# Both layers' S5 discretisation in the first steps, and the second MLP half squared on ScalarE

## What is computed

```python
proj = jnp.einsum('btd,de->bte', x, w_in)
...
mixed = jnp.concatenate([o_hg, o_rt, y5], axis=-1).astype(x.dtype) @ w_out
x = _layer_norm(ALPHA * x + mixed, ln1_w, ln1_b)
ff = jnp.square(jax.nn.relu(x @ w_up)) @ w_down
x = _layer_norm(ALPHA * x + ff, ln2_w, ln2_b)
```

```python
dt = jnp.exp(log_dt.astype(f32))[:, None]
mag = jnp.exp(dt * a_re)
ab_re = mag * jnp.cos(dt * a_im)
ab_im = mag * jnp.sin(dt * a_im)
den = a_re * a_re + a_im * a_im
nr = ab_re - 1.0
g_re = (nr * a_re + ab_im * a_im) / den
g_im = (ab_im * a_re - nr * a_im) / den
```

## Time and profile before

| | before |
|---|---|
| runs | 800.65, 802.97, 808.24 us |
| profiled execution | 800.36 us |
| its span | 798.3 us |
| TensorE matmul busy | 749.8 us (94%) |
| VectorE busy | 545.5 us (68%) |
| ScalarE busy | 380.1 us (48%) |
| mean granted TensorE clock | 0.972 |

### The profile page before, as it was taken

The page is one execution under the profiler, slowest core; times in us unless marked ns, Lnnn a source line. Parts: engine busy times, 40 slices in busy tenths (PEclk is TensorE's granted clock), DMA queues, the critical chain, the costliest instruction groups (busy, mean ns, idle before and its releaser), DMA issues.

```text
span 798.3 us, 17719 instructions
## 1 busy us (share of the span) xinstructions
PE 749.8 (94%) x7318; PEld 692.2 (87%) x7318; DVE 545.5 (68%) x1041; ACT 380.1 (48%) x727; POOL 41.9 (5%) x54
## 2 busy tenths in 40 slices
PE   5999789999999999989969899999999999999994
PEld 4888668879999999989969797778799999999994
DVE  7975872257788898884665987423478886666574
ACT  3513123435578654446448413233357874555442
POOL 4000012100000000000030001010000000000001
PEclk9999889999999999999999999999899999999998
DMA  8532122517355455444533222323354556555541
GB/s 337 188 110 79 36 71 98 211 50 221 122 159 186 159 173 194 145 151 158 166 126 106 82 82 81 123 81 114 109 171 154 176 180 187 178 169 183 186 132 55
DMA packets 31008, 113.56 MB, mean 142 GB/s; under 512 B 3568, under 2 KB 3776, under 8 KB 30544
## 3 DMA queue, kind: packets, MB, share of 16 engines
q1 hardware_dynamic: 28368, 101.83, 39.9%
q0 software_dynamic: 1984, 9.52, 3.1%
q10 hardware_dynamic: 576, 1.08, 0.4%
HBM read 108.24 MB, written 4.18 MB: 141 GB/s over the span
## 4 chain that ended last, share of the span: by engine, by line
PE 54%; DVE 21%; ACT 7%; issue 5%; DMA 1%; ACTq 0%; DVEq 0%
PE stream L998 11%; PE stream L1023 10%; PE stream L1024 10%; PE stream L1025 10%; DVE w_low L1526 8%; ACT w_high L1076 4%; PE mix L928 2%; DVE h_full L2070 1%; PE mix L899 1%; DVE h_low L2074 1%; PE mix L749 1%; ACT h_high L1418 1%; DMA w_raw<-in_weights 1%; PE mix L890 1%; PE mix L672 1%
## 5 line engine op out<-in xcount | busy, mean ns | idle before, releaser
L1526 DVE TENSOR_TENSOR w_low<-w_raw,w_high 128x1024 fp32r<-128x1024 f32 x153 | 187.3, 1224 | 92.6 <-ACT w_high L1076 91.0
L1076 ACT ACTIVATE w_high<-w_raw 128x1024 fp32r<-128x1024 f32 x153 | 161.3, 1054 | 113.3 <-PE stream L1025 94.8
L1023 PE MATMUL stream<-h_high,w_high 128*128 128x264 f32 x512 | 147.0, 287 | 1.4 <-issue 0.6
L998 PE MATMUL stream<-X,w_raw 128*128 128x264 f32 x560 | 138.1, 404 | 9.2 <-DMA w_raw<-in_weights 8.6
L1023 PE MATMUL stream<-a_high,w_high 128*128 128x264 f32 x456 | 135.3, 297 | 11.0 <-DVE a_low L2103 6.3
L1024 PE MATMUL stream<-h_low,w_high 128*128 128x264 f32 x512 | 145.1, 283 | 0.0
L1025 PE MATMUL stream<-h_high,w_low 128*128 128x264 f32 x512 | 145.0, 283 | 0.0
L998 PEld LDWEIGHTS stream<-X,w_raw 128*128 128x128 f32 x560 | 108.4, 198 | 32.2 <-DMA w_raw<-in_weights 9.0
L1024 PE MATMUL stream<-a_low,w_high 128*128 128x264 f32 x456 | 131.4, 288 | 0.0
L1025 PE MATMUL stream<-a_high,w_low 128*128 128x264 f32 x456 | 131.1, 287 | 0.0
L1023 PEld LDWEIGHTS stream<-a_high,w_high 128*128 128x128 f32 x456 | 87.8, 193 | 15.3 <-issue 14.0
(11 more groups left out here) (383 smaller groups left out, 1040.7 us busy)
## 6 DMA issues: line engine op xcount, KB each, us to landing
w_raw<-in_weights SPq DMA_DIRECT2D x192, 512.0 KB, 3.5
mats<-in_matrices POOLq DMA_DIRECT2D x2, 1024.0 KB, 5.9
S_hg<-in_state_hg POOLq DMA_DIRECT2D x2, 768.0 KB, 8.2
out_hg_s<-S_hg POOLq DMA_DIRECT2D x2, 768.0 KB, 3.7
consts<-in_constants POOLq DMA_DIRECT2D x1, 1484.5 KB, 9.4
X<-in_xT ACTq DMA_DIRECT2D x4, 264.0 KB, 5.3
out_y<-X SPq DMA_DIRECT2D x4, 264.0 KB, 2.1
S_rt<-in_state_rt POOLq DMA_DIRECT2D x2, 512.0 KB, 9.7
```

The costliest lines, as they stand in the source:

```text
L998: mm = pe.matmul(bnk[:, 0:T], w_raw[:, n % RAW_SLOTS, 128 * k:128 * k + 128], x[:, k, :], start=(kk == 0), stop=(kk == 7))
L1023: pe.matmul(bnk[:, 0:width], wh, xh, start=(first and kk == 0), stop=False)
L1076: act.activation(w_high[:, n % SPLIT_SLOTS, :], w_raw[:, n % RAW_SLOTS, :], ACT.Copy).then_inc(high_ready, 1)
L1526: put(tt(w_low[:, n % SPLIT_SLOTS, :], w_raw[:, n % RAW_SLOTS, :], w_high[:, n % SPLIT_SLOTS, :].bitcast(F32), ALU.subtract), low_ready)
```

## The change

The table `par` gets a column for each layer. The four pieces of the discretisation become a generator of their own, `s5_params`, which works on both layers at once, at twice the width, in the first steps. `s5_tables` keeps the 22 wide pieces. ScalarE's `s5_dt` and `s5_sin` are called once, at the start, for both layers; the calls in steps UP_A+3 and UP_A+12 are gone. The list of pieces has 22 places, and none in UP_A. In UP_B ScalarE makes the square itself, between relu and h_high.

```diff
-TABLE_PIECES = [UP_A + 4, UP_A + 8] + [DOWN_A + _c for _c in (2, 4, 5, 6, 8, 9, 10, 12, 13, 14)] + [UP_B + _c for _c in range(1, 15)]
+TABLE_PIECES = [DOWN_A + _c for _c in (2, 4, 6, 8, 10, 12, 14)] + [UP_B + _c for _c in range(1, 16)]
...
-        par = sb("par", [128, 20, S5_TILES])
+        par = sb("par", [128, 20, DEPTH, S5_TILES])
...
-            def s5_dt(l):
-                act.activation(par[:, 0, :], pv(l, "log_dt"), ACT.Exp).then_inc(act_params, 1)
-
-            def s5_sin(l):
-
-                act.wait_ge(par_ready, l + 1)
-                act.activation(par[:, 3:5, :], par[:, 1:3, :], ACT.Sin).then_inc(act_params, 1)
+            def s5_dt():
+                act.activation(par[:, 0, :, :], pv_both("log_dt"), ACT.Exp).then_inc(act_params, 1)
+
+            def s5_sin():
+
+                act.wait_ge(par_ready, 1)
+                act.activation(par[:, 3:5, :, :], par[:, 1:3, :, :], ACT.Sin).then_inc(act_params, 1)
...
                 act.activation(relu[:, m % 2, :], p, ACT.Relu).then_inc(relu_ready, 1)
                 copied(relu_ready, n + 1, fr)
+                act.wait_ge(h_ready, 32 * l + m - 1)
+                act.activation(h_full[:, m % 2, :], relu[:, m % 2, :], ACT.Square).then_inc(hfull_ready, 1)
                 act.wait_ge(hfull_ready, n + 1)
                 act.activation(h_high[:, m % FF_HALF, :], h_full[:, m % 2, :], ACT.Copy).then_inc(hhigh_ready, 1)
...
-                        if c == UP_A + 3 and l + 1 < DEPTH:
-                            act.wait_ge(table_ready, l + 1)
-                            s5_dt(l + 1)
-                        if c == UP_A + 12 and l + 1 < DEPTH:
-                            s5_sin(l + 1)
...
-            def s5_tables(l):
-
-                are, aim = pv(l, "a_re"), pv(l, "a_im")
-                dve.wait_ge(act_params, 2 * l + 1)
-                chain(tt(row(TH), row(DT), aim, ALU.mult))
...
+            def s5_params():
+
+                are, aim = pv_both("a_re"), pv_both("a_im")
+                dve.wait_ge(act_params, 1)
+                chain(tt(both(TH), both(DT), aim, ALU.mult))
...
-            def hidden(l, m):
-
-                n = FF_HALF * l + m - FF_HALF
-                dve.wait_ge(relu_ready, n + 1)
-                put(tt(h_full[:, m % 2, :], relu[:, m % 2, :], relu[:, m % 2, :], ALU.mult), hfull_ready)
-
...
-            first_table = s5_tables(0)
+            first_table = chained(s5_params(), s5_tables(0))
...
-                            hidden(l, c - 1 - UP_B + FF_HALF)
                             hidden_low(l, c - 1 - UP_B + FF_HALF)
```

More of the change, by code:

```diff
@@ L287, in pv, with pv_both @@
             return vecs[:, l, a:a + n]
+        def pv_both(name):
+            a, n = PV[name]
+            return vecs[:, :, a:a + n]
         ident = cv("ident")
@@ L1516, in _, with both @@
             DT, RC, RS_, COS, SIN, TH, ZR, EX, MAG, ABR, ABI, DEN, GR, GI, T0, T1, T2, PC, PS, NR = range(20)
-            def row(i):
-                return par[:, i, :]
+            def both(i):
+                return par[:, i, :, :]
             def split_low(n):
@@ L1552, in s5_tables @@
                 yield
-                chain(tt(row(ZR), row(DT), are, ALU.mult))
-                chain(ts(row(ZR), row(ZR), 1.0 / 16, None, ALU.mult))
-                chain(ts(row(EX), row(ZR), 1.0 / 8, 1.0, ALU.mult, ALU.add))
+                chain(tt(both(ZR), both(DT), are, ALU.mult))
+                chain(ts(both(ZR), both(ZR), 1.0 / 16, None, ALU.mult))
+                chain(ts(both(EX), both(ZR), 1.0 / 8, 1.0, ALU.mult, ALU.add))
                 for n in range(7, 0, -1):
-                    chain(tt(row(EX), row(EX), row(ZR), ALU.mult))
-                    chain(ts(row(EX), row(EX), 1.0 / n, 1.0, ALU.mult, ALU.add))
+                    chain(tt(both(EX), both(EX), both(ZR), ALU.mult))
+                    chain(ts(both(EX), both(EX), 1.0 / n, 1.0, ALU.mult, ALU.add))
@@ L1560, in s5_tables @@
                 yield
                 for n in range(4):
[L1562 to L1568, removed]
@@ L1578, in s5_tables @@
-                chain(tt(row(T0), row(T0), row(T1), ALU.subtract))
-                chain(tt(row(GI), row(T0), row(DEN), ALU.mult))
+                    chain(tt(both(MAG if n == 3 else EX), both(EX), both(EX), ALU.mult))
+                dve.wait_ge(act_params, 2)
+                chain(tt(both(ABR), both(MAG), both(COS), ALU.mult))
+                chain(tt(both(ABI), both(MAG), both(SIN), ALU.mult))
+                chain(ts(both(NR), both(ABR), -1.0, None, ALU.add))
+                chain(tt(both(T0), are, are, ALU.mult))
@@ new lines, in s5_params @@
+                chain(tt(both(T1), aim, aim, ALU.mult))
+                chain(tt(both(DEN), both(T0), both(T1), ALU.add))
+                chain(dve.reciprocal(both(DEN), both(DEN)))
+                yield
+                chain(tt(both(T0), both(NR), are, ALU.mult))
+                chain(tt(both(T1), both(ABI), aim, ALU.mult))
+                chain(tt(both(T0), both(T0), both(T1), ALU.add))
+                chain(tt(both(GR), both(T0), both(DEN), ALU.mult))
+                chain(tt(both(T0), both(ABI), are, ALU.mult))
@@ L1580, in s5_tables, with row @@
+                chain(tt(both(T1), both(NR), aim, ALU.mult))
+                chain(tt(both(T0), both(T0), both(T1), ALU.subtract))
+                chain(tt(both(GI), both(T0), both(DEN), ALU.mult))
                 yield
+            def s5_tables(l):
+                def row(i):
+                    return par[:, i, l, :]
                 if l == 0:
@@ L1650, in s5_tables, with chained @@
                     yield
+            def chained(*parts):
+                for part in parts:
+                    yield from part
             def run(pieces):
```

30 lines of the change are left out of this document (11 added, 19 removed).

## The result

The changed kernel takes 791.6 us (median of four runs, 789.15 to 794.43) where the kernel before takes 802.6; the ratio is 0.987, with an interval of 0.983 to 0.990. A second comparison of the same two kernels gave 791.8 us against 801.2, a ratio of 0.989 (0.985 to 0.993). The forecast was 792.6 us from 803.0, a ratio of 0.987.

What follows compares the result with a forecast made beforehand. TensorE, with work for 94% of the span, was taken as the bound. Terms 3.0 + 6.4 + 0.8 + 0.6 - 0.4 = 10.4 us took the median from 802.97 to 792.6 us, range 787.5 to 798.5.

Steps and rivals of the forecast that it cites:

- Discretisation out of UP_A: Layer 0's MLP, first stretch: without the small operations and table loads it takes layer 1's time, 3.0 us won.
- The second stretch: Rest of layer 0's MLP: square on ScalarE and pieces respaced bring 101.31 us to 94.9, 6.4 us won.
- The end of UP_B and the small table matmuls: Waits for the last h_low (0.4 us in each layer) and for a bank in layer 0 (0.6 us) go.
- The lead: How early a w_low is ready before TensorE needs it, 3.4 us; VectorE being late by less costs nothing.
- The last piece in UP_B+15: Last table piece, one step later than before, ahead of the transposes: costs nothing, covered by chunk DOWN_B, 2.90 us.
- The sine's load in DOWN_A+11: ScalarE's table load makes that step 3.4 us, 0.5 over 2.90 (1.9 late by the skill's rule), covered by 3.4 us.
- The first steps: Kernel start, VectorE: 46 operations twice as wide cost 0.4 us (other bound 2.8), on the path at 39.87.
- The partial one: Rival, UP_B and DOWN_A: part of the stalls stays, gain 7.4 to 9.4 us, median 793.5 to 795.5; 25%.
- The slower one: Rival, UP_B: ScalarE becomes the pace, each 0.1 us over 2.90 costs 3.2 us over both layers; 3%.
- The clock rival: Rival, first steps: a longer TensorE wait at 39.87 lowers the clock, costing 2.4 to 7 us, 795 to 799.6; 5%.

Runs made afterwards that it cites:

- the run with 46 more: The changed kernel with 46 more 128x16 VectorE operations in the first steps, each waited for; 803.2 us, ratio 1.001 against the kernel before.

## Why the prediction was right, point by point

*Discretisation out of UP_A.* 50.35 us was forecast and 50.26 measured. Layer 1 shows what layer 0 can reach: all kernels with this part of the change have 50.25 to 50.41. The removed operations cost 0.205 us each in a chain, start to start, not the 0.17 of their records; the sum went by the windows and was not touched.

*The second stretch.* 94.9 forecast, 94.69 measured. VectorE's wide step takes 2.90 us with 0.2 of it idle, ScalarE's 2.34 us where 2.26 was summed, and h_high never makes h_low wait. VectorE's busy time was put at 79.3 us and is 81.67: neighbouring records overlap, so 16 squares freed 4.7 us (89.39 less 84.68 in the run with the square alone), 0.29 each and not 0.43. The heading of that part credits the square and the respacing together. The runs split it: 5.3 us are the square, 1.3 the rest of the discretisation, and the respacing is worth nothing.

*The end of UP_B and the small table matmuls.* The waits of the earlier trace rows are gone:

```profile
355.05 0.28 PE L1029 MATMUL stream<-h_high,w_low 128*128 128x264 f32 x1
355.17 0.28 PE L1027 MATMUL stream<-h_high,w_high 128*128 128x264 f32 x1
...
355.41 0.28 PE L1029 MATMUL stream<-h_high,w_low 128*128 128x264 f32 x1
355.62 0.62 PE L609 MATMUL mix<-late,mats 128*32 128x128 f32 x21
```

0.12 us, where layer 0 had 0.40 as layer 1 has in the earlier trace rows, and 0.21 us, where the earlier trace rows has 0.75. Layer 1's stretch is 0.26 us shorter, close to the 0.28 that its wait was over the usual. The forecast counted the whole 0.4 in each layer, so its 0.8 was too large: with the second stretch it had 6.4 + 0.8 = 7.2 us, and 6.62 + 0.26 = 6.9 were measured. The small table matmuls gave the 0.6 that was forecast (48.74 to 48.12). In all, 10.8 us were forecast for the MLPs and what follows, and 10.7 measured. The lead needs the same care: the prediction let layer 1's lag of 2.1 us disappear in a lead of 3.4, but the last h_low has only 1.7 to 1.8, which fits the 0.28 us that the kernel before paid there.

*The last piece in UP_B+15.* Costed at nothing with chunk DOWN_B as its cover. It is nothing, but the cover was named too generously: as soon as the steps before it run late, the piece costs 2.15 us, as the kernel without the square shows, and with three squares it made TensorE wait 1.5 us. The respacing leans on the square.

*The sine's load in DOWN_A+11.* Covered, as forecast. ScalarE in that step:

```profile
288.39 1.28 ACT L1093 ACT_TABLE_LOAD   x1
289.68 1.06 ACT L1093 ACTIVATE rot<-MIX 128x1024 f32<-128x1024 f32 x1
290.65 1.04 ACT L1080 ACTIVATE w_high<-w_raw 128x1024 fp32r<-128x1024 f32 x1
```

From w_high to w_high it is 3.34 us. The Trainium skill ("ScalarE: Activation LUTs", What ACT_TABLE_LOAD costs) gives 2.66 us for a switch, with a drain of 1.38. The traces don't agree: the four added switches followed each other every 1.51 us, each with a small activation in it. An estimate from the Trainium skill's 2.66 us and the 0.21 of the activation is 11.5 us for the four; they cost 6.0.

*The first steps.* The 0.4 us are there, in the mean of the traces and on the matmul at 40.27 us. That they reach the end of the kernel can't be seen in runs that differ by several us. What failed is the check I named for them, "TensorE's wait near 39.9 longer by 0.4 us": in the profiled execution that wait is gone, because TensorE came late for another reason.

*The rivals.* The partial one would have shown h_low waiting in UP_B; it never does. The slower one needed ScalarE over 2.90 us a step, and the run with three squares shows what that costs: 2.1 to 2.25 us a layer at 0.24 us over, where the 3.2 us that I gave for each 0.1 us over both layers would make 3.8 a layer. The lead takes the first part. The clock rival was given too little weight as a mechanism. I argued from a wait of 0.67 us that the clock would stay; in the second trace TensorE waited 1.99 us there, and

```profile
40.27:46.00 5.73, 5.73 (x50) 4.41 (x51) 5.29 (x11) 0.18 (x1) 0.00 (x0) 0.70 0.13 54
```

the next 5.7 us had a clock of 0.70. The sixteen matmuls behind the wait took 5.51 us, where they take 3.83 in the traces with a clock of 1.00: 1.7 us. Whether the change has a part in that isn't shown. The length of this wait depends on when TensorE arrives: the kernel with the square alone, whose discretisation is narrow, waited 1.62 us there, and wide ones waited 1.33 to 1.92 us, all with the clock at 1.00 behind it. But some 0.4 us of the 1.99 are the change's, so it can have tipped this one execution.

What stays open is how much of the 5 us by which the MLP's start moves between executions is clock and how much is waiting for weights. No pair of runs here holds one of the two fixed.

## What to carry to other kernels

Where the same matmuls run twice in a kernel, once with a side job and once without, the undisturbed one is the forecast for the other, and it was good to 0.1 us in 50. A producer that is slower than its consumer by a fraction of a us a step costs nothing until the lead is used up, and then it is paid at the last hand-over, so read the end of the stretch first, and take the lead of that hand-over and not of another one (here 1.7 us for the last h_low against 3.4 for a w_low). Pieces placed with the least slack depend on every other step's timing: when two edits are made together, try each alone, since one may be harmless only because of the other.

## What was not expected of the hardware

A wait of 3.2 us of TensorE in the middle of the MLP cost 6.1 us: behind it the granted clock was 0.50 for 5.9 us. A wait of 2.47 us at the transposes left it at 1.00. At 40 us, waits of 1.62 us (the square alone), 1.85 us (the run without the square, new places) and 1.92 us (four more loads) were followed by a clock of 1.00, one of 1.99 us by 0.70.

In the first steps one operation of 128x16 on VectorE takes 4.75 us, in the timeline of after. GpSimd's fill of 3072 elements a partition runs beside it and ends at about the same time (13.52 us against 13.56):

```profile
8.81 4.75 DVE L1561 TENSOR_SCALAR par<-par 128x16 f32<-128x16 f32 x1
14.54 0.78 DVE L1532 TENSOR_TENSOR a_low<-X,a_high 128x264 fp32r<-128x264 f32 x2
...
10.84 2.68 POOL L531 MEMSET scratch<- 128x3072 f32 x1
```

It isn't this operation as such. In the run with 46 more, nine of them ahead of it, an earlier pass of the same loop is the long one: it starts at 8.93 and ends at 13.75 us, where the fill ends at 13.71. The kernel before has it as well, 4.92 us long. No run moves or removes the fill, so that VectorE waits for GpSimd is only argued.
